# Norms of a two-layer trunk taken by halves of the tokens, with the sum spread by a matrix of ones

## What is computed

```python
def _rmsnorm(x, gain):
    xf = x.astype(jnp.float32)
    y = xf * lax.rsqrt(jnp.mean(xf * xf, axis=-1, keepdims=True) + EPS)
    return (y * gain.astype(jnp.float32)).astype(x.dtype)
...
        def modulated(j, y):
            return _rmsnorm(y, g[j]) * (1 + mod[:, :, 3 * j + 1]) + mod[:, :, 3 * j]

        x = x + 0.5 * mod[:, :, 2] * _swiglu(modulated(0, x), ffn_w_in[l, 0], ffn_w_out[l, 0])
        h = modulated(1, x)
...
        x = x + mod[:, :, 5] * out
        x = x + 0.5 * mod[:, :, 8] * _swiglu(modulated(2, x), ffn_w_in[l, 1], ffn_w_out[l, 1])
```

## Time and profile before

| | us |
|---|---|
| median of 3 runs | 2581.17 |
| lowest and highest | 2578.25, 2582.09 |
| profiled execution | 2577.47 |
| its span in the trace | 2575.7 |
| PE busy | 2438.8 (95%) |
| DVE busy | 1520.5 (59%) |
| ACT busy | 947.5 (37%) |

### The profile page before, as it was taken

One profiled execution on the slowest core, in us unless ns is written; L12 is line 12 of the kernel. 1 busy time (PEld: TensorE's weight loads), 2 busy tenths in 40 slices (PEclk: granted clock), 3 DMA queues, 4 the chain that ended last, 5 costly groups with the idle time before them and its releaser, 6 DMA issues.

```text
span 2575.7 us, 40615 instructions
## 1 busy us (share of the span) xinstructions
PE 2438.8 (95%) x17100; PEld 2334.0 (91%) x17100; DVE 1520.5 (59%) x2397; ACT 947.5 (37%) x1438; POOL 0.2 (0%) x4
## 2 busy tenths in 40 slices
PE   6899999989798999999979999998998988999998
PEld 5899999989487899999979999998998988999998
DVE  6755646647857655646576465564334658647473
ACT  5432423324645433424354243333122235424242
POOL 0000000000000000000000000000000000000000
PEclk8999999989899999999989999998996999999999
DMA  6533543221102524524333252232220012322222
GB/s 231 160 127 123 153 142 123 90 74 50 36 18 67 179 96 139 175 90 128 110 114 124 94 188 89 64 101 64 94 68 10 1 33 66 99 66 89 76 78 78
DMA packets 252175, 251.66 MB, mean 98 GB/s; under 512 B 14978, under 2 KB 246362, under 8 KB 251994
## 3 DMA queue, kind: packets, MB, share of 16 engines
q1 hardware_dynamic: 251994, 249.08, 30.3%
HBM read 245.76 MB, written 3.28 MB: 97 GB/s over the span
## 4 chain that ended last, share of the span: by engine, by line
PE 83%; DVE 9%; ACT 4%; DMA 2%; issue 2%; SPq 0%; DVEq 0%; ACTq 0%
PE banks L830 71%; PE banks L938 2%; DMA w_raw<-ffn_w_in 1%; PE banks L1039 1%; PE banks L1041 1%; PE banks L1040 1%; DVE w_lo L1920 1%; ACT prob L1771 1%; PE banks L1115 1%; DVE z L1989 1%; ACT z L1530 1%; PE banks L1343 1%; PE banks L975 1%; DVE w_raw L1941 1%; DMA mod_grain<-w_mod 1%
## 5 line engine op out<-in xcount | busy, mean ns | idle before, releaser
L830 PE MATMUL banks<-b_hi,w_hi 128*128 128x320 f32 x2464 | 780.9, 317 | 47.2 <-DVE work L2144 17.8
L830 PE MATMUL banks<-b_lo,w_hi 128*128 128x320 f32 x2464 | 769.2, 312 | 0.0
L830 PE MATMUL banks<-b_hi,w_lo 128*128 128x320 f32 x2464 | 768.9, 312 | 0.0
L830 PEld LDWEIGHTS banks<-b_hi,w_hi 128*128 128x128 f32 x2464 | 470.1, 191 | 84.2 <-issue 68.2
L1482 ACT ACTIVATE w_hi<-w_raw 128x1024 fp32r<-128x1024 f32 x308 | 324.4, 1055 | 473.7 <-PE banks L830 308.2
L1920 DVE TENSOR_TENSOR w_lo<-w_raw,w_hi 128x1024 fp32r<-128x1024 f32 x308 | 376.8, 1224 | 192.2 <-ACT w_hi L1482 190.3
L830 PEld LDWEIGHTS banks<-b_lo,w_hi 128*128 128x128 f32 x2464 | 470.5, 191 | 0.0
L830 PEld LDWEIGHTS banks<-b_hi,w_lo 128*128 128x128 f32 x2464 | 470.0, 191 | 0.0
L830 PE MATMUL banks<-hid_hi,w_hi 128*128 128x320 f32 x1664 | 379.5, 309 | 0.0
L830 PE MATMUL banks<-hid_hi,w_lo 128*128 128x320 f32 x1664 | 379.2, 309 | 0.0
L830 PE MATMUL banks<-hid_lo,w_hi 128*128 128x320 f32 x1664 | 379.2, 309 | 0.0
(11 more groups left out here) (282 smaller groups left out, 2594.8 us busy)
## 6 DMA issues: line engine op xcount, KB each, us to landing
w_raw<-ffn_w_in SPq DMA_DIRECT2D x176, 512.0 KB, 4.8
mod_grain<-w_mod SPq DMA_DIRECT2D x256, 256.0 KB, 5.4
w_raw<-ffn_w_out SPq DMA_DIRECT2D x64, 512.0 KB, 4.4
w_raw<-ffn_w_out SPq DMA_DIRECT2D x32, 384.0 KB, 3.8
w_raw<-w_in_odd SPq DMA_DIRECT2D x20, 512.0 KB, 4.8
mod_first<-w_mod SPq DMA_DIRECT2D x4, 2048.0 KB, 16.4
w_raw<-w_in_even SPq DMA_DIRECT2D x12, 512.0 KB, 5.0
w_raw<-w_out_even SPq DMA_DIRECT2D x8, 512.0 KB, 4.1
```

Of the source, the lines that this page charges most:

```text
L830: ins = pe.matmul(o, w3[w], v3[v][cols], start=first and i == 0, stop=last and i == 2, skip_group_check=onto_read)
```

## The change

The last two output tiles ahead of a norm are taken by token halves: PE does tile 6 half 0, tile 7 half 0, tile 6 half 1, the product for the sums of half 0, tile 7 half 1 (`out_tail` behind feed-forward parts, `tail_pair` behind mixers). x is updated, squared and summed by halves. The sum over partitions is one fp32 product of 128x320 per half with a 128x128 matrix of ones, which has every row equal, so nothing is spread afterwards; root (ACT) and reciprocal (DVE) work on 128x320, once per half. In norm 0 both halves are done whole, one behind the other. DVE multiplies x by the inverse alone, and ACT applies the modulation's scale and shift in one instruction with two pointers, in pieces of 128, 192 and 320. PE takes items 0 and 2 (P1 and P2, both of half 0) first, with the second half's sums behind the second feature tile of item 0, then items 1 and 3 (`first_items_by_half`). The mixers' first products go by halves too. The grains that stood in the norms of parts 1 and 2 stand behind items 3 and 5 now. In double 0 the last sums of L2144 stand ahead of the weight sum for double 1 in all four parts.

```diff
-            def sum_squares(n):
-
-                pe.wait_ge(square_added, KT * (n + 1))
-                for t in range(TT):
-                    ins = pe.matmul(token_sums[:, t:t + 1], ss[:, t * P:(t + 1) * P], ones[:, 0:1], start=True, stop=True)
-                ins.then_inc(sums_ready, 1)
-
-            def spread_inverse(n):
-
-                pe.wait_ge(inverse_ready, n + 1)
-                for t in range(TT):
-                    dst = inverse_of[0] if t == 0 else inverse_of[1][:, (t - 1) * P:t * P]
-                    ins = pe.matmul(dst, rms[:, t:t + 1].to_broadcast([P, P]), ident[:, :], start=True, stop=True)
-                ins.then_inc(inverse_spread, 1)
-
-            def ffn(f, halfway=None):
+            def half_sums(n, hf):
+
+                pe.wait_ge(square_added, half_squares(n, hf))
+                if n > 0 and hf == 1:
+                    pe.wait_ge(rms_ready, 2 * n + 1)
+                pe.matmul(bank[SUM_BANK + (hf if n == 0 else 0)][:, 0:HALF], ones[:, :], ss[:, half_of(hf)], start=True, stop=True)\
+                    .then_inc(sums_ready, 1)
+
+            def out_part(f, c, u, hf):
+
+                n, q = CHUNKS[c], out_slot(c, u)
+                for k in range(n):
+                    ins = split_product([(bank[out_banks(u)[hf]][:, 0:HALF], (slice(None), half_of(hf)))],
+                                        (ring_out(w_hi, q, n)[:, k, :], ring_out(w_lo, q, n)[:, k, :]),
+                                        (hid_hi[:, k, :], hid_lo[:, k, :]), k == 0, k == n - 1)
+                return ins
+
+            def out_tail(f, c, n):
+
+                for u in (KT - 2, KT - 1):
+                    pe.wait_ge(lo_ready, out_ev(f, c, u) + 1)
+                    pe.wait_ge(x_updated, out_base(f) + KT * c + u - 1)
+                    out_part(f, c, u, 0).then_inc(tail_part, 1)
+                out_part(f, c, KT - 2, 1).then_inc(w_used, 1)
+                half_sums(n, 0)
+                out_part(f, c, KT - 1, 1).then_inc(w_used, 1)
...
+            def first_items_by_half(f, n, x_count):
+
+                for k in range(HK):
+                    item_step(f, 0, k)
+                    if k == 1:
+                        half_sums(n, 1)
+                pe.wait_ge(x_updated, x_count)
+                for k in range(HK):
+                    pe.wait_ge(form_lo[2], form_done(f, 2, k))
+                    if k == 0:
+                        pe.wait_ge(lo_ready, in_ev(f, 0, 2) + 1)
+                    for s in range(2):
+                        item_part(0, 2, s, k)
+                for k in range(HK):
+                    item_step(f, 1, k)
...
-                    order = [(t, kt) for kt in range(KT) for t in range(4)] + order[4 * KT:]
+                    order = [(t0 + i, kt) for t0 in (0, 2) for kt in range(KT) for i in range(2)] + order[4 * KT:]
                 for t, kt in order:
                     if kt == 0:
                         taken(fill0 + t)
-                    if fresh is not None and t == 0:
-                        pe.wait_ge(h_lo_ready, KT * MIX_NORMS.index(fresh) + kt + 1)
+                    if fresh is not None and t == 0 and kt == HK:
+                        half_sums(fresh, 1)
+                    if fresh is not None and t in (0, 2):
...
+            def root(n, hf):
+
+                act.wait_ge(sums_ready, 2 * n + hf + 1)
+                act.activation(ss[:, half_of(hf)], bank[SUM_BANK + (hf if n == 0 else 0)][:, 0:HALF], ACT.Sqrt, scale=1.0 / D,
+                               bias=eps[:, 0:1]).then_inc(rms_ready, 1)
+
+            def shift_half(n, view, kt, hf):
 
                 l, j = divmod(n, N_SUB)
-                root(n)
-                keep_ctx_inverse(n)
-                split_hi(unit, "mix")
+                act.wait_ge(scaled_ready, scaled_done(n, kt, hf))
+                for v, cols in HALF_PIECES[hf]:
+                    ins = act.activation(view[:, cols], view[:, cols], ACT.Identity, scale=mod_col(v, l, 3 * j + 1, kt),
+                                         bias=mod_col(v, l, 3 * j, kt))
+                ins.then_inc(z_ready, 1)
+                act.wait_ge(z_ready, scaled_done(n, kt, hf))
...
-            def scale_x(n, kt, dst):
-
-                l, j = divmod(n, N_SUB)
-                for v, cols in PARTS:
-                    ins = dve.scalar_tensor_tensor(out=dst[:, cols], in0=x[:, kt, cols], scalar=mod_col(v, l, 3 * j + 1, kt),
-                                                   in1=(ctx_inverse if v == 0 else inverse_of[1])[:, :], op0=ALU.mult, op1=ALU.mult)
-                ins.then_inc(scaled_ready, 1)
...
+            def invert(n, hf):
+
+                dve.wait_ge(rms_ready, 2 * n + hf + 1)
+                dve.reciprocal(ss[:, half_of(hf)], ss[:, half_of(hf)]).then_inc(inverse_ready, 1)
+
+            def scale_half(n, view, kts, hf):
+
+                dve.wait_ge(inverse_ready, 2 * n + hf + 1)
+                inverse = ss[:, half_of(hf)].unsqueeze(1).to_broadcast([P, kts.stop - kts.start, HALF])
+                dve.tensor_tensor(view, x[:, kts, half_of(hf)], inverse, ALU.mult).then_inc(scaled_ready, kts.stop - kts.start)
+
+            def tail_norm(n, last_half, scale, low, middle):
+
+                add_sq_half(n, KT - 2, 0)
+                add_sq_half(n, KT - 1, 0)
+                middle()
+                last_half(KT - 2)
+                invert(n, 0)
+                scale(slice(0, 1), 0)
+                add_sq_half(n, KT - 2, 1)
+                scale(slice(1, 2), 0)
+                low(slice(0, 1), 0)
+                scale(slice(2, 4), 0)
+                last_half(KT - 1)
+                low(slice(1, 2), 0)
+                add_sq_half(n, KT - 1, 1)
+                scale(slice(4, 6), 0)
+                low(slice(2, 4), 0)
...
+                tail_norm(n, last_half, scale, low, middle)
+                invert(n, 1)
+                item_lo(f, 0, 2)
+                scale(slice(6, 8), 0)
+                low(slice(4, 6), 0)
+                weight_sum(f, 0, 2)
+                scale(slice(0, 1), 1)
+                low(slice(6, 8), 0)
+                scale(slice(1, 2), 1)
+                first_sum(slice(0, 1))
...
-                else:
+                elif d > 0:
                     weight_sum(f, d + 1, 0)
                 for s in range(2):
                     part_done(f, d, 5, s)
                     dve.wait_ge(p5_kept, n + s + 1)
                     dve.tensor_tensor(work[:, s, 2, :], work[:, s, 2, :], role(d, s, "A"), ALU.add).then_inc(c22_done, 1)
-                    if not last:
+                    if not last and d > 0:
                         if s == 0:
                             item_lo(f, d + 1, 1)
                         else:
                             weight_sum(f, d + 1, 1)
+                if d == 0:
+                    weight_sum(f, d + 1, 0)
+                    item_lo(f, d + 1, 1)
+                    weight_sum(f, d + 1, 1)
                 if last:
```

More of the change, by code:

```diff
@@ L987, in ffn @@
                     if last_of_chunk(d):
-                        for u in range(KT):
+                        tail = d == DOUBLES - 1 and norm_after is not None
+                        for u in range(KT - TAIL if tail else KT):
                             out_unit(f, chunk_of(d), u)
+                        if tail:
+                            out_tail(f, chunk_of(d), norm_after)
             def first_out_pair(unit, early, late, banks_free, late_ready):
@@ new lines, in first_norm, with shifted @@
+            def first_norm(n, f, keep_rows):
+                l, j = divmod(n, N_SUB)
+                sqrt_table()
+                for hf in range(2):
+                    root(n, hf)
+                def shifted(kt):
+                    act.wait_ge(scaled_ready, kt + 1)
+                    for v, cols in PARTS:
+                        ins = act.activation(z[:, kt, cols], z[:, kt, cols], ACT.Identity, scale=mod_col(v, l, 3 * j + 1, kt),
+                                             bias=mod_col(v, l, 3 * j, kt))
@@ L2196, in ffn @@
                     final = d + 1 == DOUBLES
-                    for u in range(KT):
+                    tail = final and after[0] is not None
+                    for u in range(KT - TAIL if tail else KT):
                         update_x(out_ev(f, c, u), l, 2 * h, u, out_banks(u))
@@ L2649, in _ @@
             item_lo(0, 0, 1)
-            invert(0)
+            for hf in range(2):
+                invert(0, hf)
             def keep_first(n):
```

478 lines of the change are left out of this document (328 added, 150 removed).

## The result

| | before | changed kernel |
|---|---|---|
| median, us | 2579.71 | 2609.72 |
| lowest and highest, us | 2573.81, 2582.09 | 2605.72, 2612.44 |
| profiled execution, us | 2577.47 | 2612.44 |

The change makes the kernel slower: ratio 1.0119, 95% interval 1.0096 to 1.0141, about 31 us. The forecast was 2590.7 with a range up to 2603, so the sign was right and the size a third of what came.

A forecast was written before the change was run, and what follows sets the result against it. The prediction took TensorE, busy 95% of the span, as the bound; its norm terms 0.5 + 3.0 - 0.8 + 2.7 + 3.3 + 0.8 = +9.5 us, against 2581.17, gave 2590.7 us, range 2576 to 2603.

The forecast's parts named there:

- norm 0: Norm at the start: scaling some 2 us later for roots and reciprocals, eight scalings 1.5 shorter, +0.5 us.
- the walk of the norm: Instruction-by-instruction timing of one norm, each engine in written order, time 0 at tile 6's products; good to about 0.2 us.
- norm 3: Norm ahead of a feed-forward part: item 0 6.0 us earlier, item 6 at 59.8 against 57.1, +2.7 us.
- norm 4: Norm ahead of a mixer: 16 half steps for eight, +3.6 us less 0.3 for the clock, +3.3.
- norm 1: Norm ahead of a mixer: 16 half steps for eight, +3.5 us less 0.5 for the clock, +3.0.
- norm 2: Norm behind a mixer, ahead of a feed-forward part: item 6 at 61.3 against 61.2, later products 0.9 shorter, -0.8 us.
- norm 5: Norm behind a mixer, ahead of a feed-forward part: item 6 at 61.3 against 60.6, with 0.1 for the clock +0.8 us.
- Rivals 1 and 4: Long-row reciprocal on DVE: fast at 0.40 us, total 2576.5, chance 0.08; or slow at 2.6, total 2597, chance 0.08.
- rival 2: ACT's second pointer is free: five norms each give back 1.4 us, total 2583.6, chance 0.15.
- Rival 3: PE stays at 1.2 GHz through the broken items: mixers 5 us later each, total 2605, chance 0.12.
- Rival 5: Weight work holds DVE, so item 0 stays at 21 and all behind is 4 to 6 later: 2610, chance 0.04.
- the sentence on item 6: Weights for item 1 of double 1: split ends at 63.5, wanted at 66.8, so no cost.

The follow-up runs named there:

- e7: Changed kernel with ACT's shift reading only the bias pointer, the modulation's scale left out: 2600.00 us, ratio to before 1.0094.
- e6: Changed kernel with double 1's modulation grains loaded ahead of the weights of double 2: 2592.54 us, ratio to before 1.0067.
- e4: Changed kernel with its twelve 128x320 reciprocals replaced by an elementwise maximum, the inverse left out: 2588.55 us, ratio to before 1.0046.
- e5: Kernel before with the new order of double 0 and double 1's grains loaded ahead of double 2's weights: 2566.12 us, ratio 0.9954.
- e9: Changed kernel with cheap passes for reciprocals, one pointer in the shift and double 1's grains loaded ahead of double 2's weights: 2564.87 us, ratio to before 0.9958.
- e2: Kernel before with the new order of double 0 alone: 2577.61 us, ratio to before 1.0002.

## Why the prediction was wrong

**Right, mostly to the tenth.** The reciprocal at 6 ns per element (forecast 2.1 us, measured 2.146), the second pointer (forecast 0.09, measured 0.092; the first one is 122 ns by the forecast's own two rows, 278 and 400, more than the 0.09 that it took from them), the walk of the norm: in norm 3 item 0 at 15.2 (walk 15.2), the two reciprocals at 10.4 and 20.4 (10.5 and 20.2), item 5 at 50.8 (50.6), item 6 at 60.1 (59.8), though PE's wait ahead of it was 3.0 and not 4.6. Norm 3 costs 3.0 up to item 6 (forecast 2.7), norm 4 with its mixer's start 3.1 (3.3), norm 1 with the whole even mixer 3.6 (3.0), norm 2 up to item 6 0.1 (0.1), norm 5 0.7 (0.7). Rivals 1 and 4 on the reciprocal fall with that, as does rival 2 (the pointer isn't free: e7). Rival 3, the low clock, isn't needed: 0.82 in the stretch above against 0.86 before. Rival 5 falls with item 0's start.

**Wrong: everything behind item 6.** The step that failed is the sentence on item 6 that the weights of item 1 in double 1 "cost nothing". It looked at one load and at its own deadline. It didn't follow SP's queue one load further, to the grains that stand behind the weights of double 2, nor the buffers whose release the moved weight sums delay. In the table the changed kernel loses 7.7 us between item 6 of part 0 and double 2, 4.5 behind item 6 of part 1, 2.8 and then 2.6 in part 2, and 5.0 in part 3: 22.6 us that the sum had at 0, -0.9, 0 and 0.1. Even the 0.9 came (12.0 late at item 6 of part 1, 11.2 one item on) before it was lost again. e6 takes back 13 us in all.

**Wrong in its working: norm 0.** Forecast +0.5, for a later item 0 and shorter scalings. Item 0 is 3.1 late and item 5 4.3. At item 6 it is 0.6, but that is luck: the new order takes away PE's wait of 3.6 for it, which the sum for norm 0 didn't count. The 1.5 us that shorter scalings were to give back didn't come. With the cheap pass (e4) the 3.1 is -0.1, so it is the reciprocals; without the second pointer (e7) it stays 3.1, so it isn't that.

**The account.** Reciprocals 19, second pointer 6.5, queue 13: together 39. Against them stands what the new order of double 0 is worth once the queue is mended, 10 to 12 (e5), and halves that give nothing (e9 against e5). That leaves 27 to 29, measured 31; each term is uncertain by 4 to 7 us, by the intervals, so that the agreement is no finer than that. The reciprocals' 19 is more than the walk's 14; the intervals of the two runs leave room for both.

**What comes late where there are no grains.** Behind item 6 of part 3 the changed kernel loses 5.0 us. No run was made for it, but the traces tell where it goes (changed kernel, double 2 of part 3, DVE and then PE):

```profile
2239.11 1.23 DVE L2124 TENSOR_TENSOR w_raw<-w_raw 128x1024 f32<-128x1024 f32 x1 [2.69 <-DMA w_raw<-ffn_w_in]
```

```profile
2240.88 0.38 PE L872 MATMUL banks<-b_hi,w_hi 128*128 128x320 f32 x1 [1.93 <-DVE work L2430]
```

The weights themselves are late there: the weight sum waits for their DMA, the sums for item 6 stand behind it, and PE waits 1.93. The 1.8 late in part 2 is the same. All nine traces with the new order of double 0 lose between item 6 and 2264 (1.3 to 5.0 us; e5 2.1, e2 3.1), the four others with the old order don't (-1.0 to 0.2). So the order of double 0 costs something there too, and grains first doesn't mend it: e6 loses 4.2. **Open:** why that loss is 5.0 in one trace and 1.3 in another.

## What to carry to other kernels

When an instruction that frees a buffer moves, follow the DMA queue from that buffer's next load to everything queued behind it, up to its use: a load with a late buffer holds up loads whose buffers are free, and putting those ahead made a change that was worth nothing alone worth 10 us. Take reciprocals before a value is spread: 5 elements per partition cost 0.19 us where the spread row of 320 costs 2.15. Work brought forward in pieces to an engine that waits for two others in step started earlier here and ended no earlier (in norm 3 item 0 six us earlier, item 4 three us later).
